# Unread products on TensorE between the last eight units of expert weights

## The reference

```
def expert_choice_ffn(h, router, w_gate, w_up, w_down):
    cap = CAPACITY_FACTOR * S // N_EXPERTS
    aff = jax.nn.softmax(jnp.einsum('bsd,de->bse', h, router), axis=-1)
    vals, idx = lax.top_k(aff.transpose(0, 2, 1), cap)
    xg = jax.vmap(lambda hb, ib: hb[ib])(h, idx)
    hid = jax.nn.silu(einsum('becd,edf->becf', xg, w_gate)) * einsum('becd,edf->becf', xg, w_up)
    y = einsum('becf,efd->becd', hid, w_down) * vals[..., None]
    return zeros((S, D)).at[idx].add(y)          # per sequence
...
x = x + expert_choice_ffn(rms_norm(x, norm_ffn), router, exp_gate, exp_up, exp_down)
return rms_norm(x, norm_final)
```

## Time and profile before

| | |
|---|---|
| three runs | 1758.36, 1760.07, 1760.36 us |
| the profiled execution: its time | 1760.31 us |
| the profiled execution: its span | 1758.5 us |
| mean granted TensorE clock | 0.941 of full |
| TensorE busy | 1587.2 us, 90% of the span |
| transfers | 386.35 MB, mean 220 GB/s |
| weight transfers in slices 32 to 39 of 40 | 420 to 422 GB/s |

### The profile page before, as it was taken

The page is one execution under the profiler, slowest core; times in us unless marked ns, Lnnn a source line. Parts: engine busy times, 40 slices in busy tenths (PEclk is TensorE's granted clock), DMA queues, the critical chain, the costliest instruction groups (busy, mean ns, idle before and its releaser), DMA issues.

```text
span 1758.5 us, 25942 instructions
## 1 busy us (share of the span) xinstructions
PE 1587.2 (90%) x10710; PEld 1077.5 (61%) x10710; DVE 802.2 (46%) x1622; ACT 372.9 (21%) x941; POOL 2.2 (0%) x6
## 2 busy tenths in 40 slices
PE   8999999999999999999999999999999767667665
PEld 5877878884488786888648778888853112101111
DVE  5676567565577765766656575242421000000001
ACT  4262131110325422311002561111211000000001
POOL 0000000000000000000000000000000000000000
PEclk9999999999999999999999999999999867777777
DMA  9314325354542242544444232221878999999997
GB/s 393 126 73 145 143 106 222 144 191 167 202 169 96 95 170 72 195 181 157 180 173 162 102 102 116 74 75 51 346 323 351 422 420 421 420 422 420 421 421 320
DMA packets 55520, 386.35 MB, mean 220 GB/s; under 512 B 6256, under 2 KB 6768, under 8 KB 10480
## 3 DMA queue, kind: packets, MB, share of 16 engines
q1 hardware_dynamic: 53424, 375.16, 54.1%
q10 hardware_dynamic: 1984, 9.57, 1.4%
HBM read 383.65 MB, written 1.05 MB: 219 GB/s over the span
## 4 chain that ended last, share of the span: by engine, by line
PE 72%; DMA 22%; DVE 3%; ACT 2%; issue 1%; SPq 0%; DVEq 0%; ACTq 0%
PE ps L205 53%; DMA arena<-in_stream 15%; DMA ring<-in_stream 6%; PE ps L2313 3%; PE ps L1063 2%; PE ps L1552 2%; PE ps L209 1%; PE ps L1162 1%; PE ps L713 1%; PE ps L1195 1%; PE ps L1221 1%; PE ps L1653 0%; PE ps L614 0%; PE ps L1003 0%; PE ps L2395 0%
## 5 line engine op out<-in xcount | busy, mean ns | idle before, releaser
L205 PE MATMUL ps<-arena 128*128 128x256 f32 (+4 forms) x2364 | 539.8, 492 | 72.5 <-DMA arena<-in_stream 62.8
L205 PEld LDWEIGHTS ps<-arena 128*128 128x128 f32 (+1 forms) x2364 | 304.2, 170 | 267.2 <-DMA arena<-in_stream 141.7
L205 PE MATMUL ps<-ring,arena 128*128 128x256 f32 (+5 forms) x1172 | 323.9, 499 | 34.7 <-DMA ring<-in_stream 30.2
L205 PE MATMUL ps<-arena,ring 128*128 128x256 f32 (+1 forms) x1212 | 274.4, 374 | 0.0
L205 PEld LDWEIGHTS ps<-ring,arena 128*128 128x128 f32 (+1 forms) x1172 | 177.9, 174 | 155.2 <-issue 70.5
L205 PEld LDWEIGHTS ps<-arena,ring 128*128 128x128 f32 x1212 | 216.2, 191 | 35.5 <-issue 9.6
L2649 PE MATMUL ps<-arena 128*32 128x512 f32 x218 | 147.3, 780 | 0.0
L2871 DVE TENSOR_TENSOR arena<-arena,ps 128x512 f32<-128x512 f32 x8 | 5.5, 687 | 307.5 <-PE ps L2649 307.5
L1110 ACT ACTIVATE arena<-arena,small 128x256 f32<-128x256 f32 x112 | 55.7, 498 | 69.6 <-DVE small L1097 53.2
L1699 ACT ACTIVATE arena<-arena 128x512 f32<-128x512 f32 x20 | 12.6, 630 | 179.4 <-DVE arena L1755 179.4
L1063 PE MATMUL ps<-arena 64*128 64x256 f32 (+3 forms) x256 | 46.8, 392 | 0.8 <-DVE arena L1093 0.5
(11 more groups left out here) (458 smaller groups left out, 1975.6 us busy)
## 6 DMA issues: line engine op xcount, KB each, us to landing
arena<-in_stream SPq DMA_DIRECT2D x160, 1024.0 KB, 24.4
ring<-in_stream SPq DMA_DIRECT2D x155, 1024.0 KB, 6.4
spare<-in_stream SPq DMA_DIRECT2D x16, 1024.0 KB, 26.5
par<-in_stream SPq DMA_DIRECT2D x8, 1024.0 KB, 27.0
const<-in_stream SPq DMA_DIRECT2D x8, 1024.0 KB, 26.5
par<-in_layer_par ACTq DMA_DIRECT2D x3, 1664.0 KB, 7.3
par<-in_stream SPq DMA_DIRECT2D x8, 512.0 KB, 25.4
const<-in_stream SPq DMA_DIRECT2D x8, 512.0 KB, 24.7
```

Source lines behind the costliest of these rows:

```text
L205: ins = self.pe.e.matmul(out, lhsT, rhs, start=start, stop=stop)
```

## The change

After each of the first three units of a quarter TensorE gets four unread products, after the fourth two; each multiplies the identity by `back` (256 columns, float32) into the dead bank. That is 3 x 4 + 2 = 14 for a quarter and 28 in all. None has a wait or a signal, and nothing reads the bank.

```
+TAIL_IDLE = 4
...
@@ quarter_product
         if j < KC // 2 - 1:
             ins.then_inc(w.free, 1)
+            tail_idle_pe(p, pe, TAIL_IDLE)
     w.used()
     ins.then_inc(tiles.full, 1)
+    tail_idle_pe(p, pe, TAIL_IDLE // 2)
+
+
+def tail_idle_pe(p, pe, n):
+
+    for _ in range(n):
+        pe.e.matmul(p.gather_banks[0][:, 0:NB, :], p.c("ident"), p.back)
```

## The result

Twelve runs of the changed kernel took 1762.82 to 1766.85 us, median 1764.72; twelve of the kernel before, beside them, 1758.07 to 1761.82, median 1759.87. The ratio is 1.0028, 95% interval 1.0020 to 1.0036: 4.85 us slower by the medians, or 3.5 to 6.3 by the interval, over the 0.2% that was to count as a change. The profiled execution took 1766.39 us, span 1764.6.

What follows compares the result with a forecast made beforehand. Weight landings bound the kernel, plus a tail of about 8 us; products make TensorE the chain: 3.60 us of lateness, -0.87 + 0.24, and -0.52 give +2.45 on 1760.31, so 1762.7 us, range 1760.7 to 1766.0.

Steps and rivals of the forecast that it cites:

- the products fitted: Rival, chance 0.03: unread products cost the path nothing, u7 starts on its landing at full clock, end 1.2 us earlier, 1759.1.
- cheap: Rival, chance 0.14: identity weight loads hidden and switches costing little, +0.6 to +1.2 us, 1760.9 to 1761.5.
- switch: Between a unit's narrow weights and the products' full-width weights on TensorE: 0.11 us there and 0.08 back.
- half clock on entry: Rival, chance 0.28: u0 meets 1.2 GHz and the product chain runs slower, 1763.6 to 1766.1 us.
- What bounds, and that landings stay: Kernel's end is the last weight landing plus a tail of about 8 us; the change moves no transfer.
- A product, 0.43 us: Each unread float32 product on TensorE at full clock is two passes of 0.216 us, 0.43 us.
- The unit with four products, 2.82 us: In the last two quarters: 0.90 + 0.11 + 1.73 + 0.08 us, against data every 2.48 us.
- Two products ahead of `added` outlast the copy: After u3 and u7, products take 1.87 us against 1.63 for ScalarE's copy, so `added` waits 0.24 us more.
- u0 at 1731.78 and full clock from there: Start of the second half's units: u0 begins as before at 1731.78 us and TensorE stays at full clock.
- the prediction's own sign: In u0 to u3: passes of 0.43 us there would show the forecast wrong.
- T: Time at half clock after 1731.8 us, costing T/2; from 1.8 us on it decides for slower by over 0.2%.
- The gain of a warm array, 1.2 us: At u7 and the last `added`, full clock in place of half can give back 0.65 + 0.52 = 1.2 us.

Runs made afterwards that it cites:

- the changed kernel's second profile: The changed kernel run again with no edit: six runs, median 1764.52 us, ratio 1.0033; the profiled execution took 1763.92 us.
- its second profile: The kernel before, run again with no edit for another profile, which had half clock on entry and at the end: 1760.88 us.
- the second series: Six more runs of the changed kernel with no edit: 1763.91 to 1767.29 us, median 1764.52, ratio 1.0033.
- the three in which the products fit: Changed kernel with fewer products and pairs in the first half: full-width once (median 1759.23 us), narrow in two series (1758.99 and 1759.06).

## Why the prediction was right and where it was wrong

The time is inside the range, and the chain of products is what happens: u7 doesn't start on its landing, as it would if the products fitted, and they are not cheap either. But the likeliest outcome, no measurable change (given 0.67, on a sum of 2.45 us), is not what was measured. Two things stand behind the difference: a switch that costs more than its term, and half clock on entry, which was a rival given 0.28.

- **What bounds, and that landings stay:** right. The landing is at 1727.94 us where it was 1728.08, the last weights move in the same stretch (16 GB/s from 1747 to 1748 us in both profiles, none in the us after it), and no unit waits for them.
- **A product, 0.43 us:** right, from 28 more of them.
- **The unit with four products, 2.82 us:** it is 2.93. The step that failed is the switch, taken at 0.11 + 0.08 us. The 0.11 is the distance to the start of the first full-width pass, and that is there (u1 to the products 1.00 us, of which 0.90 is the unit). But the first such pass itself steps by 0.32 us and not 0.216:

```profile
1738.60 0.70 PE L2682 MATMUL ps<-arena,const 128*128 128x256 f32 x2
...
1738.92 0.59 PE L2682 MATMUL ps<-arena,const 128*128 128x256 f32 x2
```

The load of the second pass's weights ends at 1738.90, 0.02 us ahead of that pass, which fits that its weights were not loaded ahead either; that this is the reason is not shown. The row of before had the price: its `added` takes 1.06 us for four passes, and I had used 0.94. Six steps make 0.64 us of what the forecast lacked, and the two places ahead of `added` 0.10 each: u3 to `added` is 1.97, not 1.87.
- **Two products ahead of `added` outlast the copy:** right in kind; 0.34 us each time in place of 0.24, a third of it given back because `added` finds its weights loaded. Together: u0 to addition was forecast at 22.34 us and is 23.08, and 0.64 + 0.20 - 0.11 is 0.73 of the 0.74.
- **u0 at 1731.78 and full clock from there:** true for the execution that was profiled before, and for the changed kernel's second profile (3.70 us after the landing in both). For its first profile it is false, and so by the prediction's own sign: u0 begins there with passes 0.43 us apart (1734.30 to 1734.73 to 1735.15). At full clock the sum is 35.45 - 32.23 = 3.2 us, against 2.45 forecast, which the switch explains.
- **Half clock on entry:** the mechanism was right, the place wrong. I counted T from u0 on. But the last unit of the first half (0.86 us more) and its `added` (1.80 more) lie on the same chain, and cost the changed kernel 2.66 us before u0 has begun. In the kernel before they are absorbed, which its second profile shows. That the rival's 1766.1 us comes near the 1766.39 of the profiled execution is in part luck: its 3.4 us stood for 6.8 us at half clock from u0 on, and u0 met only about 0.8 us of it, at a cost of 0.37. Half clock on entry stood in 6 of the 9 profiles whose first half has no unread products, and half clock for the first part in one more. A mix of 3.2 and 6.2 by that share gives 5.2 us and one to one 4.7; 4.85 was measured, and its interval, 3.5 to 6.3, holds both. The twelve times fall in two groups, seven from 1762.82 to 1764.97 and five from 1766.34 to 1766.85; the six of the second series (1763.91 to 1767.29) don't part so clearly. So the share of the executions at half clock is worked out, not measured by run.
- **The gain of a warm array, 1.2 us:** it is there, and it is 1.4. The 0.65 in its sum is the difference of two rows' lengths (1.50 and 0.85); from start to start, u7 to `added` was 2.50 us where u3 to `added` was 1.63, so 0.87, which the sum of the change does use. With the 0.52 of `added` it is 1.39. From u7 to the addition it is 3.76 us in the profile before and 2.37 or 2.38 in the three in which the products fit; one of these, 31.04 us, has u7's data 0.17 later. With four products at full clock the gain is outweighed by 4.6 (3.2 + 1.4).

The clock was forecast at its level from one execution, although the page showed both levels in that stage; the price of the worse level belonged in the likeliest case. The Trainium skill, "TensorE: Matmul & The Clock Gate" (HAM oscillation), says that waits for data between bursts of matmuls send the clock down, and that it stays up where they are closed. The trace of the changed kernel agrees, with 2.4 GHz from 1735.5 us to the end of TensorE's work. The fall at 1747.2 us before, which the prediction took as agreeing, is weaker support: waits of 1.2 to 1.4 us stood ahead of u2, u3, u5 and u6 as well, and there the clock stayed at 2.4 GHz.

## What to carry to other kernels

Idle time ahead of a transfer that paces the kernel is also the reserve with which a late engine catches up. Filler work has to leave part of it. Here, of the 2.48 us between landings, four products of full width (2.93 us with the unit) made TensorE the bound, three (2.49) left no reserve, and two (2.06) left 0.4 us a unit, too little for u7 to reach its landing after half clock on entry. Two narrow ones (1.73, an estimate: 0.86 + 2 x 0.43) left waits of 0.5 us ahead of u6 and u7; as both profiles of them had full clock on entry, how fast they recover from a drop is not shown. A gain in the whole time is shown for none of them. Where the clock has two levels, price a change at both, and from the point where the chain begins, not where the edit does.

## What was not expected of the hardware

- Going from 32-column weights to 128-column weights and back costs 0.34 us a round (2.93 against 2.59 us). The forecast's 2.82 had 0.23 of it: 0.11 before the first pass, 0.08 after the last, and 0.04 in its 0.90 for the unit, which takes 0.86 between narrow products.
- A filler of four narrow products side by side costs no more time on TensorE than one of full width, 0.43 us (1.73 us for four sets of them, and 11.98 us for 28 products of full width), and no switch.
